# A quarter of the last stage's row gathers split in two by bounded indices, on one NeuronCore

## The chip, the cores and the metric

The kernel runs on one core of a Trainium2 chip. The metric is the device time of one launch in microseconds (us). A profiled execution also gives the span from the first to the last instruction. The core has TensorE (PE), VectorE (DVE), ScalarE (ACT), GpSimd (POOL) and SyncE (SP), and 16 DMA engines that all queues share.

## The reference

A two-layer transformer with dilated and windowed attention and expert-choice experts is followed by a second one of two layers, each with a mixer and a retrieval layer over 16,384 single-neuron experts. The part that matters here is that retrieval layer, in its second layer, for the second half of the 256 tokens:

```python
def peer_ffn(h, w_q, sub_keys, u, v):
    q = (h @ w_q).reshape(b, s, PEER_HEADS, 2, PEER_QDIM // 2)
    scores = jnp.einsum('bshic,ikc->bshik', q, sub_keys).astype(jnp.float32)
    top_s, top_i = lax.top_k(scores, PEER_TOPK)                 # 16 of 128 keys, twice
    ...
    cand_i = top_i[..., 0, :, None] * PEER_KEYS + top_i[..., 1, None, :]
    ...
    best_s, pos = lax.top_k(cand_s, PEER_TOPK)
    expert = jnp.take_along_axis(cand_i, pos, axis=-1)
    gate = jax.nn.softmax(best_s, axis=-1).astype(h.dtype)
    ...
        act = jax.nn.gelu(jnp.einsum('td,thkd->thk', xt, u[et]), approximate=False)
        return jnp.einsum('thk,thkd->td', act * gt, v[et])
```

Each token has 8 heads of 16 experts, that is 128 experts; an expert is a row of `u` and a row of `v`, 1024 floats each. An expert's number is `128 * a + b`, a and b being its two keys.

## The kernel before

The rows of `u` and `v` lie side by side in one tensor `puv` of 32,768 rows (16,384 of each layer) of 2048 floats, 8 KB. The 128 tokens of a tile stand on the 128 partitions. There are four gather stages, `(l, i)`: layer l, tile i. A stage handles 128 sets j. Set j is one row for each token, the row of its j-th expert: one indirect DMA issued by POOL brings 128 rows, 1 MB, with the row numbers in column j of `IX[:, i]`. For each set

- POOL (`gather`, L3167) waits until TensorE has used the buffer's former set (`.used`), and issues the gather;
- VectorE (L2465) waits for the landing (`g{l}{i}.{j}`) and multiplies the `u` half with the token's activations to one number;
- ScalarE (L2529) makes the gelu, times the gate, and spreads it over a diagonal matrix `dg`;
- TensorE (L1610) waits for `g` and `dg` and adds `dg` times the `v` half to the accumulators `acc` in four matmul instructions.

All four take the sets in the order of j. The sets go round through a `Ring` of buffers. At set 90 of the first stage the ring comes to hold buffers 0 to 7 alone, so that eight sets of 1 MB stand in turn in eight buffers from there on. Each buffer k has a semaphore `rows_landed[k]`.

The row numbers come from `route(l, i, q)`, 13 steps on VectorE between the sets of the quarter before; the row numbers of quarter q serve sets 32q to 32q+31. In the last stage `(1, 1)` its only side work is the routing of the next quarter and a short end of tile 0. After set 127 `final_last` adds the accumulators, normalises and stores. `did` adds to an engine's own semaphore, `land` sets up a DMA's landing as a name to wait for:

```python
                    k, before = rows.take(name)
                    G.wait_ge(*at[f"{before}.used"])
```

Of the kernel before, what the change touches and what calls it, by code (L numbers as in the profile page):

```python
# [6 lines left out]
U32 = mybir.dt.uint32  # L7
# [122 lines left out]
def program(nc, I, out):  # L130
    ctx = ExitStack()
    with ctx:
        def sb(name, shape, dt=F32):
            return ctx.enter_context(nc.sbuf_tensor(name, shape, dt))
# [11 lines left out]
        cbuf = sb("cbuf", [P, 2, 1536])  # L146
        ar = sb("ar", [P, 16384])
        bc = sb("bc", [P, 324])
        arU = ar[:, :].bitcast(U32)
        PS = [ctx.enter_context(nc.psum_tensor(f"ps{i}", [P, 512], F32)) for i in range(8)]  # L150
        zd = nc.dram_tensor("zd", (12, 128, 512), F32, kind="Internal").ap()
# [40 lines left out]
        def arv(a, b, pat=None, **k):  # L192
            v = ar[:, a:b]
            return v if pat is None else v.rearrange(pat, **k)
# [278 lines left out]


        GA = arv(6656, 6912, "p (i n) -> p i n", i=2)
        IX = arU[:, 6912:7168].rearrange("p (i n) -> p i n", i=2)
        DT = arv(7168, 7424, "p (i n) -> p i n", i=2)
        DG = arv(7424, 7936, "p (k n) -> p k n", k=4)
# [1156 lines left out]
        def vector_program(V):  # L1635
# [6 lines left out]
            def ts(o, i, s1, s2, op0, op1, *names):  # L1642
                if op1 is None:
                    V.did(V.e.tensor_scalar(o, i, s1, None, op0), *names)
                else:
                    V.did(V.e.tensor_scalar(o, i, s1, s2, op0, op1), *names)  # L1646
# [755 lines left out]
            def route(l, i, q):  # L2402
                p = f"rt{l}{i}{q}"
                yield
                yield
                V.wait_ge(*at[p + ".out"])
                for c in range(4):
                    top16(TS[:, c, :], TIU[:, c, :], SS[:, c, :], R2[:, 0:128])
                    yield
                copy(TIF, TIU, p + ".ss")  # L2410
                t4 = TS.rearrange("p (h i) n -> p h i n", i=2)
                tt(CA.rearrange("p h (a b) -> p h a b", a=16), t4[:, :, 0, :].unsqueeze(3).to_broadcast([P, 2, 16, 16]),
                   t4[:, :, 1, :].unsqueeze(2).to_broadcast([P, 2, 16, 16]), ALU.add)
                yield
                for h in range(2):
                    top16(BS[:, h, :], PO[:, h, :], CA[:, h, :], R2[:, 0:256])
                    yield
                gi = GA[:, i, 32 * q:32 * q + 32].rearrange("p (h n) -> p h n", h=2)
                tt(gi, BS, BS[:, :, 0:1].to_broadcast([P, 2, 16]), ALU.subtract, p + ".gi")
                ts(PQ[:, 0], PO, 4, None, ALU.logical_shift_right, None)  # L2420
                ts(PQ[:, 1], PO, 15, None, ALU.bitwise_and, None)
                copy(PQF, PQ)
                yield
                f4 = TIF.rearrange("p (h i) n -> p h i n", i=2)
                io = C("iota")[:, 0:16].unsqueeze(1).unsqueeze(1).to_broadcast([P, 2, 16, 16])
                e4 = EQ.rearrange("p (h k a) -> p h k a", h=2, k=16)
                for n in range(2):
                    tt(e4, PQF[:, n].unsqueeze(3).to_broadcast([P, 2, 16, 16]), io, ALU.is_equal)
                    tt(e4, e4, f4[:, :, n, :].unsqueeze(2).to_broadcast([P, 2, 16, 16]), ALU.mult)
                    red(I12[:, n], e4, ALU.add)  # L2430
                    yield
                stt(I12[:, 0], I12[:, 0], 128.0, I12[:, 1], ALU.mult, ALU.add)
                ts(IX[:, i, 32 * q:32 * q + 32].rearrange("p (h n) -> p h n", h=2), I12[:, 0], float(l * 16384), None,
                   ALU.add, None, p + ".ix")
                gates_of(p, gi)
                yield

# [681 lines left out]
        def pool_program(G):  # L3119
# [33 lines left out]
            def gather(l, i):  # L3153
                for j in range(128):
                    if (l, i, j) == (0, 0, 90):
                        for k in (10, 11):
                            rows.keep(k)
                        rows.release_first(6, 7)
                    if (l, i) == (0, 0) and j in (0, 16):
                        G.wait_ge(*at[f"rt000.ix{j // 16}"])  # L3160
                    elif j % 32 == 0:
                        G.wait_ge(*at[f"rt{l}{i}{j // 32}.ix"])
                    name = f"g{l}{i}.{j}"
                    k, before = rows.take(name)
                    G.wait_ge(*at[f"{before}.used"])
                    place[name] = k
                    G.land(G.e.indirect_dma_start(  # L3167
                        out=rows_of(name), out_offset=None, in_=I["puv"],
                        in_offset=bass.IndirectOffsetOnAxis(ap=IX[:, i, j:j + 1], axis=0)), rows_landed[k], count, name)
                    if (l, i) == (0, 0) and j in NEAR_AT:  # L3170
                        hp = NEAR_AT[j]
                        G.wait_ge(*at[f"ma1.bh{hp}"])
                        G.wait_ge(*at["ma1.mask"])
                        masked(1, hp, aB1[hp % 2])
# [179 lines left out]
```

## Time and profile before

| | |
|---|---|
| device time, median of 2 runs (lowest, highest) | 3018.68 us (3015.69, 3021.68) |
| span of the profiled execution | 3014.0 us |
| median less span | 4.7 us |
| busy: TensorE, VectorE, ScalarE, POOL | 82%, 47%, 29%, 23% |
| bytes moved, mean rate | 1103.07 MB, 366 GB/s |
| gathers: number, bytes, packets | 512, 536.90 MB, 73,728 |
| last gather issued, last instruction group | 2986.94 us, 3010.86 us |

The busy shares are means over the whole span. The time that the profiled execution itself took beside its span isn't recorded apart; the table sets the median against it. What the change touches lies in the last stage, which ends the kernel. It has 128 of the 512 gathers.

### The profile page before, as it was taken

To read this page: it belongs to the slowest core of one execution; us is meant where nothing else is said; L and a number is where in the kernel's file an instruction comes from. 1 tells how busy PE (TensorE), PEld (TensorE's weight loads), DVE (VectorE), ACT (ScalarE), POOL (GpSimd) and SP (SyncE) were. 2 spreads that over 40 slices of the span, in tenths; PEclk is the share of its full clock that TensorE was granted. 3 is DMA by queue.
4 is the path that set the end of the run, shared out by engine and by line. 5 is a ranking of instruction groups with operands and counts; after the bars stand their busy time and mean duration, and the time that the engine had idled before them with its cause. 6 is when DMAs were issued, how large, how long until landed. Compare 5 with 4: busy or idle time off the path is not lost.

```text
span 3014.0 us, 33710 instructions
## 1 busy us (share of the span) xinstructions
PE 2483.8 (82%) x11942; PEld 1357.6 (45%) x11942; DVE 1427.4 (47%) x3388; ACT 875.9 (29%) x2346; POOL 705.6 (23%) x626
## 2 busy tenths in 40 slices
PE   8999865657999966656798999898897988977777
PEld 8777311112978421212475445464462644632222
DVE  3363100002355201000448886687766787676674
ACT  0231100000022100000225554357334663344333
POOL 4020000001311000000014553334334334444442
PEclk9999978778999987888899999999999999999999
DMA  6337999999434899999929999999999999999997
GB/s 262 141 135 307 413 428 429 427 428 420 175 114 160 368 427 427 427 428 428 381 93 416 419 417 420 421 422 404 411 422 422 422 373 422 421 421 421 421 421 326
DMA packets 123511, 1103.07 MB, mean 366 GB/s; under 512 B 13744, under 2 KB 19280, under 8 KB 23760
## 3 DMA queue, kind: packets, MB, share of 16 engines
q1 hardware_dynamic: 47888, 560.88, 44.7%
q0 software_dynamic: 73728, 536.90, 43.2%
q10 hardware_dynamic: 1728, 3.14, 0.3%
q8 instruction: 95, 1.56, 0.2%
q14 instruction: 72, 0.59, 0.1%
HBM read 1096.68 MB, written 4.19 MB: 365 GB/s over the span
## 4 chain that ended last, share of the span: by engine, by line
PE 41%; DMA 41%; DVE 10%; issue 4%; ACT 3%; POOL 1%; SPq 0%; DVEq 0%; ACTq 0%
PE ps L771 17%; DMA wbuf<-in_puv,ar 17%; PE ps L1610 11%; DMA wbuf<-in_w_expert_up 9%; DMA wbuf<-in_w_expert_down 7%; DMA wbuf<-in_w_expert_gate 6%; PE ps L962 4%; PE ps L1142 3%; DVE wbuf L2465 3%; DMA wbuf<-in_w_mem_kv 2%; PE ps L927 2%; ACT ar L2529 2%; PE ps L775 1%; ACT L2529 1%; DVE ar L1640 1%
## 5 line engine op out<-in xcount | busy, mean ns | idle before, releaser
L1610 PE MATMUL ps<-wbuf,ar 128*128 128x512 f32 x1960 | 935.4, 617 | 181.5 <-ACT ar L2529 181.0
L2465 DVE CUSTOM_DVE_ANT_0 wbuf<-wbuf,Y 128x1024 f32<-128x1024 f32 x490 | 603.3, 1231 | 344.3 <-DMA wbuf<-in_puv,ar 335.4
L3167 POOL DMA_INDIRECT wbuf<-in_puv,ar x490 | 549.5, 1121 | 809.0 <-PE ps L1610 728.0
L1142 PE MATMUL ps<-wbuf,ar 128*32 128x512 f32 x2944 | 456.9, 757 | 288.3 <-DMA wbuf<-in_w_expert_up 112.5
L1610 PEld LDWEIGHTS ps<-wbuf,ar 128*128 128x128 f32 x1960 | 360.2, 195 | 674.1 <-issue 671.9
L2529 ACT ACTIVATE ar<-ar 128x1 f32<-128x1 f32 (+1 forms) x1051 | 269.5, 256 | 656.2 <-DVE ar L2465 635.0
L771 PE MATMUL ps<-HT,wbuf 128*128 128x128 f32 (+1 forms) x2640 | 411.3, 312 | 7.4 <-DMA wbuf<-in_w_mem_kv 5.9
L771 PEld LDWEIGHTS ps<-HT,wbuf 128*128 128x128 f32 x2640 | 373.3, 192 | 60.9 <-issue 26.6
L1142 PEld LDWEIGHTS ps<-wbuf,ar 128*32 128x32 f32 x2944 | 92.6, 125 | 639.3 <-issue 204.5
L2526 ACT COPY ar<-ps 128x512 f32<-128x512 f32 (+4 forms) x166 | 76.3, 460 | 705.8 <-PE ps L1142 304.0
L3126 POOL TENSOR_TENSOR sm<-sm,co 128x1 f32<-128x1 f32 x18 | 10.5, 583 | 1111.8 <-DVE sm L1646 1111.6
L1640 DVE TENSOR_TENSOR ar<-ar,ps 128x512 f32<-128x512 f32 (+1 forms) x20 | 13.2, 660 | 464.2 <-PE ps L1142 462.9
L2529 ACT ACTIVATE ar<-co,ar 128x128 f32<-128x128 f32 x512 | 205.6, 401 | 21.6 <-PE ps L1610 5.0
L1637 DVE COPY ar<-ps 128x512 f32<-128x512 f32 (+5 forms) x76 | 47.1, 620 | 335.5 <-PE ps L1142 270.4
L2529 ACT ACT_TABLE_LOAD x101 | 129.6, 1283 | 91.1 <-PE ps L1142 53.0
L3141 POOL TENSOR_TENSOR wbuf<-wbuf 128x512 f32<-128x512 f32 x20 | 26.2, 1308 | 343.9 <-DMA wbuf<-in_w_branch_b 214.1
L771 PE MATMUL ps<-ar 64*128 64x256 f32 (+3 forms) x508 | 97.3, 390 | 9.9 <-DVE ar L1637 7.1
L2529 ACT ACTIVATE ar<-ar,sm 128x257 f32<-128x257 f32 (+2 forms) x84 | 45.8, 545 | 163.1 <-issue 56.2
L771 PEld LDWEIGHTS ps<-ar 64*128 64x128 f32 (+1 forms) x508 | 55.8, 191 | 64.1 <-issue 41.3
L2529 ACT ACTIVATE ar<-ps 128x512 f32<-128x512 f32 (+2 forms) x43 | 20.8, 484 | 218.1 <-PE ps L1142 191.0
L771 PE MATMUL ps<-wbuf,HT 128*128 128x256 f32 (+1 forms) x384 | 83.4, 369 | 0.0
L962 PE MATMUL ps<-wbuf 128*128 128x128 f32 x640 | 77.9, 275 | 0.0
(208 smaller groups left out, 2089.6 us busy)
## 6 DMA issues: line engine op xcount, KB each, us to landing
wbuf<-in_w_expert_down SPq DMA_DIRECT2D x64, 2048.0 KB, 31.8
wbuf<-in_w_expert_up SPq DMA_DIRECT2D x62, 2048.0 KB, 31.4
wbuf<-in_w_expert_gate SPq DMA_DIRECT2D x58, 2048.0 KB, 30.7
wbuf<-in_w_in SPq DMA_DIRECT2D x20, 2048.0 KB, 9.0
wbuf<-in_peer_w_q SPq DMA_DIRECT2D x14, 2048.0 KB, 11.9
wbuf<-in_b_w_in SPq DMA_DIRECT2D x6, 2048.0 KB, 11.8
wbuf<-in_w_o SPq DMA_DIRECT2D x5, 2048.0 KB, 23.1
wbuf<-in_w_branch_b SPq DMA_DIRECT2D x4, 2048.0 KB, 7.6
```

What stands on the lines that cost most here:

```text
L771: m = T.e.matmul(o, l, r, start=(n == 0), stop=(n == len(pairs) - 1))
L775: return T.e.transpose(o, i, ident[0:i.shape[0], 0:i.shape[0]])
L927: m = T.e.matmul(b[:, :], lhs[:, c, 128 * i:128 * i + 128], v[:, c, :], start=(c == 0), stop=(c == 7))
L962: m = T.e.matmul(o, l[:, c, :], r[:, c, :], start=(start and c == 0), stop=(c == 3), skip_group_check=True)
L1142: m = T.e.matmul(ps(jobs[n])[32 * k:32 * k + 32, :], lhs(c, k), v[:, 512 * n:512 * n + 512], start=(c == 0), stop=(c == 7), tile_position= ...
L1610: m = T.e.matmul(acc[n][:, :], DG[:, j % 4, :], rows_of(name)[:, 1024 + 512 * n:1536 + 512 * n], start=(j == 0), stop=(j == 127))
L1637: V.did(V.e.tensor_copy(o, i), *names)
L1640: V.did(V.e.tensor_tensor(o, a, b, op), *names)
L2465: V.did(V.e.tensor_tensor_reduce(u, u, Y[:, i, :], 1.0, 0.0, ALU.mult, ALU.add, DT[:, i, j:j + 1]), f"dot{l}{i}.{j}")
L2526: A.did(A.e.copy(o, i), *names)
L2529: A.did(A.e.activation(o, i, f, **kw), *names)
L3167: G.land(G.e.indirect_dma_start(out=rows_of(name), out_offset=None, in_=I["puv"], in_offset=bass.IndirectOffsetOnAxis(ap=IX[:, i, j:j + 1] ...
```

## The change

Only stage `(1, 1)` changes. Its sets with j = 0, 4, 8, ... (32 of 128) are brought by two gathers into the same buffer. Both are given a bound, 32,767, with the order to leave out, without an error, a row whose number is above it. The first, "far", reads its numbers from `IX`, where 65,536 has been added to the rows whose second key b is below 24. The second reads them from `NX`, where 65,536 has been added to all others. So each row of the set comes by one of them. The other 96 sets come by one gather each, as before, with the true numbers, now in `FX`. `NX` and `FX` are columns of a new tile `near_ix`.

POOL issues in the order far j, j+1, j+2, near j, j+3. Ahead of near j it waits until far j has landed. The name `g11.j`, for which VectorE and TensorE wait, now stands for the landing of near j. The routing of the four quarters makes seven small results in place of one.

```diff
+        near_ix = sb("near_ix", [P, 256])
...
+        NX, FX = (near_ix[:, a:a + 128].bitcast(U32) for a in (0, 128))
...
                 stt(I12[:, 0], I12[:, 0], 128.0, I12[:, 1], ALU.mult, ALU.add)
-                ts(IX[:, i, 32 * q:32 * q + 32].rearrange("p (h n) -> p h n", h=2), I12[:, 0], float(l * 16384), None,
-                   ALU.add, None, p + ".ix")
+                ix = IX[:, i, 32 * q:32 * q + 32].rearrange("p (h n) -> p h n", h=2)
+                if (l, i) == (1, 1):
+                    ts(FX[:, 32 * q:32 * q + 32].rearrange("p (h n) -> p h n", h=2), I12[:, 0], 16384.0, None, ALU.add, None)
+                    far = R2[:, 0:32].rearrange("p (h n) -> p h n", h=2)
+                    ts(far, I12[:, 1], 24.0, 65536.0, ALU.is_lt, ALU.mult)
+                    tt(I12[:, 1], I12[:, 0], far, ALU.add)
+                    ts(ix, I12[:, 1], 16384.0, None, ALU.add, None)
+                    ts(far, far, -1.0, 65536.0, ALU.mult, ALU.add)
+                    tt(I12[:, 1], I12[:, 0], far, ALU.add)
+                    ts(NX[:, 32 * q:32 * q + 32].rearrange("p (h n) -> p h n", h=2), I12[:, 1], 16384.0, None, ALU.add, None,
+                       p + ".ix")
+                else:
+                    ts(ix, I12[:, 0], float(l * 16384), None, ALU.add, None, p + ".ix")
...
                     place[name] = k
...
+                    if (l, i) == (1, 1) and j % 4 == 0:
+                        late = (j, k, name)
+                        G.land(G.e.indirect_dma_start(
+                            out=rows_of(name), out_offset=None, in_=I["puv"],
+                            in_offset=bass.IndirectOffsetOnAxis(ap=IX[:, i, j:j + 1], axis=0),
+                            bounds_check=32767, oob_is_err=False), rows_landed[k], count, name + ".far")
+                        continue
+                    if (l, i) == (1, 1):
+                        G.land(G.e.indirect_dma_start(
+                            out=rows_of(name), out_offset=None, in_=I["puv"],
+                            in_offset=bass.IndirectOffsetOnAxis(ap=FX[:, j:j + 1], axis=0)), rows_landed[k], count, name)
+                        if j % 4 == 2:
+                            j0, k0, first = late
+                            G.wait_ge(*at[first + ".far"])
+                            G.land(G.e.indirect_dma_start(
+                                out=rows_of(first), out_offset=None, in_=I["puv"],
+                                in_offset=bass.IndirectOffsetOnAxis(ap=NX[:, j0:j0 + 1], axis=0),
+                                bounds_check=32767, oob_is_err=False), rows_landed[k0], count, first)
```

On POOL, a quarter of the last stage stands like this before; L3167 is the gather, `tensor_done` the wait for the buffer, `vector_done` that for the row numbers:

```order
L3167 DMA wbuf<-in_puv,ar 128x2048 [waits tensor_done,vector_done]
L3167 DMA wbuf<-in_puv,ar 128x2048 [waits tensor_done] x31
L3167 DMA wbuf<-in_puv,ar 128x2048 [waits tensor_done,vector_done]
L3167 DMA wbuf<-in_puv,ar 128x2048 [waits tensor_done] x31
L3167 DMA wbuf<-in_puv,ar 128x2048 [waits tensor_done,vector_done]
```

The same place afterwards, in the midst of a quarter; L3182 is a far gather, L3188 a whole one, L3194 a near one:

```order
L3182 DMA wbuf<-in_puv,ar 128x2048 [waits tensor_done]
L3188 DMA wbuf<-in_puv,near_ix 128x2048 [waits tensor_done] x2
L3194 DMA wbuf<-in_puv,near_ix 128x2048 [waits rows_landed2]
L3188 DMA wbuf<-in_puv,near_ix 128x2048 [waits tensor_done]
L3182 DMA wbuf<-in_puv,ar 128x2048 [waits tensor_done]
L3188 DMA wbuf<-in_puv,near_ix 128x2048 [waits tensor_done] x2
L3194 DMA wbuf<-in_puv,near_ix 128x2048 [waits rows_landed0]
```

Each four sets have five gathers, and the fourth of them stands behind a wait for a landing.

On VectorE, at the end of a routing, the row numbers before; L2465 is a set's product (two rows each), L1649 joins the two keys, L1652 begins the gates:

```order
L2465 ISA wbuf,ar<-wbuf,Y 128x1024 [waits rows_landed1,vector_done]
L2465 ISA ar 128x1
L1649 SCALAR_TENSOR_TENSOR ar<-ar 128x32 [waits vector_done]
L1644 TENSOR_SCALAR ar<-ar 128x32 [waits vector_done]
L1652 TENSOR_REDUCE sm<-ar 128x2 [waits scalar_done,vector_done]
```

and afterwards:

```order
L2478 ISA wbuf,ar<-wbuf,Y 128x1024 [waits rows_landed1,vector_done]
L2478 ISA ar 128x1
L1651 SCALAR_TENSOR_TENSOR ar<-ar 128x32 [waits vector_done]
L1646 TENSOR_SCALAR near_ix<-ar 128x32 [waits vector_done]
L1648 TENSOR_SCALAR ar<-ar 128x32 [waits vector_done]
L1642 TENSOR_TENSOR ar<-ar 128x32 [waits vector_done]
L1646 TENSOR_SCALAR ar<-ar 128x32 [waits vector_done]
L1648 TENSOR_SCALAR ar<-ar 128x32 [waits vector_done]
L1642 TENSOR_TENSOR ar<-ar 128x32 [waits vector_done]
L1646 TENSOR_SCALAR near_ix<-ar 128x32 [waits vector_done]
L1654 TENSOR_REDUCE sm<-ar 128x2 [waits scalar_done,vector_done]
```

Six instructions more stand there, four times in the kernel. The orders of TensorE, ScalarE and SP have no other row than before.

## Rows read from the trace of the kernel before

**Rows 1.** The page: DMA share and GB/s, 40 slices; transfer queues.

```profile
DMA  6337999999434899999929999999999999999997
GB/s 262 141 135 307 413 428 429 427 428 420 175 114 160 368 427 427 427 428 428 381 93 416 419 417 420 421 422 404 411 422 422 422 373 422 421 421 421 421 421 326
...
q0 software_dynamic: 73728, 536.90, 43.2%
```

**Rows 2.** Engines in 260 us of the last gather stage.

```profile
core 0: us, PE busy (x) PEld busy (x) DVE busy (x) ACT busy (x) POOL busy (x), PEclk, DMA share, GB/s
2700.00:2960.00 260.00, 198.18 (x429) 73.27 (x430) 180.65 (x395) 102.41 (x321) 112.00 (x105) 1.00 1.01 421
```

**Rows 3.** Chain that ended last, last stage, one turn of the buffers.

```profile
2962.40 1.29 DVE wbuf L2465
...
2963.79 0.21 ACT ar L2529
...
2964.35 0.41 ACT ar L2529
...
2964.90 1.97 PE ps L1610 x4
...
2967.12 15.02 DMA wbuf<-in_puv,ar
```

**Rows 4.** Gathers of the last stage: durations, then issue to landing.

```profile
L3167 POOL DMA_INDIRECT wbuf<-in_puv,ar x116: 932/939/1985, 2698.3 to 2986.9; - x116
...
  PE ps L1610: 161.8, 102
  issue: 4.0, 13
...
DMA to landing us min/median/max: 13.6/15.1/16.1
```

**Rows 5.** Timeline of POOL, last quarter of the last stage.

```profile
start us, us, engine line op out<-in xcount [idle before <-releaser]
...
2937.27 0.94 POOL L3167 DMA_INDIRECT wbuf<-in_puv,ar  x1 [1.56 <-PE ps L1610]
2939.75 0.94 POOL L3167 DMA_INDIRECT wbuf<-in_puv,ar  x1 [1.54 <-PE ps L1610]
```

**Rows 6.** First and fifth gather of a burst into an empty queue.

```profile
L3167 POOL DMA_INDIRECT wbuf<-in_puv,ar x1: 1125/1125/1125, 1573.4 to 1573.4; - x1
...
DMA to landing us min/median/max: 5.7/5.7/5.7
...
L3167 POOL DMA_INDIRECT ar<-in_puv,ar x1: 937/937/937, 1578.7 to 1578.7; - x1
...
DMA to landing us min/median/max: 11.8/11.8/11.8
```

**Rows 7.** Three gathers issued into a thin queue, stage before.

```profile
L3167 POOL DMA_INDIRECT wbuf<-in_puv,ar x3: 939/941/1039, 2476.8 to 2481.0; - x3
...
DMA to landing us min/median/max: 6.6/7.6/7.7
```

**Rows 8.** Timeline at the end: last set, last products.

```profile
2986.94 0.94 POOL L3167 DMA_INDIRECT wbuf<-in_puv,ar  x1 [1.49 <-PE ps L1610]
...
3002.02 1.22 DVE L2465 CUSTOM_DVE_ANT_0 wbuf<-wbuf,Y 128x1024 f32<-128x1024 f32 x1 [1.23 <-DMA wbuf<-in_puv,ar]
...
3003.35 0.53 ACT L2529 ACTIVATE ar<-ar 128x1 f32<-128x1 f32 x2 [1.49 <-DVE ar L2465]
3003.91 0.40 ACT L2529 ACTIVATE ar<-co,ar 128x128 f32<-128x128 f32 x1
...
3004.45 1.96 PE L1610 MATMUL ps<-wbuf,ar 128*128 128x512 f32 x4 [0.50 <-ACT ar L2529]
...
3006.52 1.41 DVE L1640 TENSOR_TENSOR X<-X,ps 128x512 f32<-128x512 f32 x2 [3.26 <-PE ps L1610]
```

**Rows 9.** VectorE groups of the last stage by shape.

```profile
L1644 DVE TENSOR_SCALAR ar<-ar 128x32 uint32<-128x32 uint32 x6 | 1.4, 231 | 0.2
...
L1640 DVE TENSOR_TENSOR ar<-ar 128x32 f32<-128x32 f32 x3 | 0.6, 192 | 0.1
...
L1644 DVE TENSOR_SCALAR ar<-ar 128x32 uint32<-128x32 f32 x3 | 0.5, 181 | 0.1
```

**Rows 10.** TensorE before, where its clock had fallen; then those stretches.

```profile
2472.71 5.37 PE L1610 MATMUL ps<-wbuf,ar 128*128 128x512 f32 x8 [1.71 <-ACT ar L2529]
...
2472.00:2473.00 1.00, 0.29 (x1) 0.30 (x2) 0.96 (x3) 0.90 (x4) 0.00 (x0) 0.98 1.02 434
2473.00:2474.00 1.00, 1.00 (x2) 0.34 (x1) 0.93 (x4) 0.90 (x4) 0.00 (x0) 0.50 1.14 352
2476.00:2477.00 1.00, 1.00 (x3) 0.53 (x2) 1.00 (x2) 0.00 (x0) 0.17 (x1) 0.81 0.58 221
```

More of the change, by code:

```diff
@@ L3166, in gather @@
                     place[name] = k
-                    G.land(G.e.indirect_dma_start(
-                        out=rows_of(name), out_offset=None, in_=I["puv"],
-                        in_offset=bass.IndirectOffsetOnAxis(ap=IX[:, i, j:j + 1], axis=0)), rows_landed[k], count, name)
+                    if (l, i) == (1, 1) and j % 4 == 0:
[16 more added lines that the diff above has]
+                                bounds_check=32767, oob_is_err=False), rows_landed[k0], count, first)
+                    else:
+                        G.land(G.e.indirect_dma_start(
+                            out=rows_of(name), out_offset=None, in_=I["puv"],
+                            in_offset=bass.IndirectOffsetOnAxis(ap=IX[:, i, j:j + 1], axis=0)), rows_landed[k], count, name)
                     if (l, i) == (0, 0) and j in NEAR_AT:
```

## The prediction

> **What bounds the kernel now.** I read the page's rows of transfers first. Over the last tenth the DMA engines are full in nearly every slice, at 421 GB/s [rows 1]. The windows of the last stage then say whether that is its limit: the DMA share is 1.01, TensorE is busy 198 of 260 us with its clock at 1.00, VectorE 181 and POOL 112 [rows 2]. So a set costs what its bytes cost: 1,048,576 B at 421 GB/s is 2.49 us, and POOL's issues do stand 2.48 us apart [rows 5]. The chain shows how this closes into a ring: gather issued, 15.0 us to landing, product on VectorE 1.29, ScalarE 0.21 and 0.41 with a small gap, TensorE 1.97, next gather [rows 3]. From that product's start (2962.40) to the gather (2967.12) are 4.7 us, and with the 15.0 such a turn takes 19.7 us: eight sets of 2.48. POOL waits for TensorE 102 times, 161.8 us in all [rows 4]: it stands behind the buffers, not the buffers behind it. Of the 15.1 us from issue to landing the transfer is 2.49, so that most of it is queue. A gather into an empty queue landed after 5.7 us [rows 6]. The cover of the stage, the time by which an issue may be late without an idle DMA engine, is thus about 15.1 - 5.7 = 9.4 us.
>
> **What the change does to the transfers.** The bytes stay the same if a row that is left out moves nothing. With b spread evenly over 128 keys (my assumption), 24/128 of a split set, 0.19, comes late: 0.47 us of transfer for near and 2.02 for far. The transfers already fill the engines, so nothing here can shorten them; I exclude a gain beyond run-to-run spread. What may be added is four things.
>
> First, **more gathers**, 160 in place of 128. A gather has 73,728 / 512 = 144 packets, 16 more than its 128 rows [rows 1]. What these 16 and the gather's end cost can't be seen alone. The nearest rows are rates: loads of 2 MB run at 428 GB/s, gathers of 1 MB at 421 [rows 1], or 2.45 against 2.49 us for 1 MB. If all of that difference is the gather's own cost, it is 0.04 us, and 32 more cost 1.3 us.
>
> Second, **the wait for far j**. Here the cover goes. Call W the time when far j has landed. Then only j+1 and j+2 are in the queue. Without a gap the landings would come at W+2.5 (j+1), W+5.0 (j+2), W+5.4 (near j), W+7.9 (j+3), W+10.0 (far j+4): a group of four takes 9.96 us. POOL's smallest gap between two gathers is 0.30 us and a gather takes it 0.94 [rows 4, 6]. So near j starts at W+0.3, j+3 at W+1.5, far j+4 at W+2.8, j+5 at W+4.0, j+6 at W+5.3. Their buffers are free by then: set j-4, the latest to become complete, had its near part landed 4.5 us before W and needs 2.5 us to TensorE [rows 3] and 2 us there; from there TensorE frees one buffer each 2 us. The critical one is j+3, issued 6.4 us before it should land. The fastest landing on record is 5.7 us, from an empty queue [rows 6]; into a thin queue three took 6.6, 7.6 and 7.7 [rows 7]. With 5.7 there is no loss. With 6.6 it is 0.2 us, with 7.7 it is 1.3 us a group. POOL's own time adds to it: its gathers take 0.94 us at the median but up to 1.99 [rows 4], and the mean, 112.00 us for 105 in the window, is 1.07 [rows 2]. Two issues stand on the path after W, so +0.3. I take the fastest of the thin queue, since j+1 and j+2 still run when j+3 is issued, and the mean of POOL: 0.2 + 0.3 = 0.5 us a group, 32 x 0.5 = 16 us. From both sides: 0, and the burst of rows 6. There the fifth gather, issued 5.3 us after the first, landed 11.4 us after it, so four landings took 11.4 for 9.96, 1.4 us lost a group, 46 us in all. A bounded gather may also take POOL longer than 0.94; nothing shows it. Each 0.1 us more in near costs up to 3 us.
>
> On the fixed part of a DMA the trace says that it lies under the queue while there is one: 5.7 us alone, 2.49 in a row [rows 2, 6]. The Trainium skill, page "DMA: Bandwidth & Descriptors", section "Anatomy of one DMA — SWDGE (gpsimd) path", fits a DMA as about 2.0 us plus its bytes over 436 GB/s, most of the first in the receipt of the last write. Its section "Rules for kernel authors" asks for 1 MiB in a DMA and for small ones to be joined, which speaks against this change. If those 2.0 us lay bare for each added gather, they would be an estimated 64 us in place of my 16 + 1.3; rows 2 speak against that as long as gathers queue.
>
> Third, **the order of completion**. VectorE and TensorE take the sets in order, so j, j+1, j+2 are all taken after near j lands, one set late for j+1, two for j. TensorE needs 4 x 1.96 = 7.8 us in 9.96 [rows 8] and catches up within the group. At the end there is no later group. Before, the last set's product starts at 3002.02, the matmuls at 3004.45 and end at 3006.41, 4.4 us later [rows 8]. Now near 124 lands one set, 2.49 us, ahead of set 127, and four sets have still to pass: -2.49 + 2.43 + 4 x 1.96 = 7.8. The tail grows by 3.4 us.
>
> Fourth, **24 small VectorE instructions** of 32 columns, 0.18 to 0.23 us each [rows 9], 5 us in all, six at a time. VectorE is idle 79 of 260 us [rows 2]; behind them are queued one product and the gates. The row numbers are wanted when the buffer of 8 sets before is free; they are made at the 26th set of a quarter and wanted for the 33rd, whose buffer is that of the 25th: about when POOL, after its new wait, reaches that set. The six, 1.2 us, fit in the 2.8 us that stand between W and far j+4. Cost 0. Were that cover gone, four times 1.2.
>
> Sum: 3014.0 + 1.3 + 16 + 3.4 = 3034.7 us of span. The median of the runs stands 4.7 above the span of before. Predicted: **3039 us**.
>
> **The rivals.**
>
> *The queue never runs thin.* If a loaded queue hands j+3 through like the empty one, only 1.3 + 3.4 remain: 3014.0 + 4.7 + 4.7 = 3023 us. For it: 5.7 us as lowest; against it: rows 7, and POOL's long issues.
>
> *Each group starts as from an empty queue.* Then the burst's 46 us: 3014.0 + 1.3 + 46 + 3.4 + 4.7 = 3069. For it: far j, being the slowest engine's landing, leaves the engines that had few of its rows ahead, with even less queued. Against: two whole sets are in the queue at W.
>
> *A left-out row costs like one that is brought* (slower than 2%). The place is the DMA queue, in each split set: its 128 rows are handled twice. Price 32 x 2.49 = 80 us: 3023 + 80 = 3103, more with thin queues. It passes 2% (60 us) as soon as, with my other 20.7, a left-out row costs half a whole one. No row shows a left-out row, for or against. I count with it the case in which the fixed part lies bare: by the two rates it is 32 x (5.7 - 2.49) = 103 us at the utmost, 3014.0 + 103 + 3.4 + 4.7 = 3125, and the skill's 2.0 us gives an estimate of 3086.
>
> *TensorE becomes the bound through its clock.* After an idle of 1.71 us the granted clock fell to 0.50 (of 2.4 GHz, so 1.2) for about 3 us, and two sets took 5.37 in place of 3.92 [rows 10]. The change gathers TensorE's gaps of half a us, now four in a group, into one of about 2 us. One such spell a group gives 7.8 + 1.5 = 9.3 us, still under 9.96, so it costs only its part in the tail, 1.5 us. If it stayed low throughout, 15.7 us a group, 32 x 5.7 = 182 us: 3200. Against: with two sets and more at hand, TensorE runs without a gap, and the clock was back at 1.00 within 4 us there.
>
> **How the numbers follow.** Thin queue with a loss of 0.2 to 1.2 us a group (3029 to 3062): 0.52, its middle at 3039. Never thin (3017 to 3029): 0.22. As from empty (3062 to 3079): 0.10. Over 3079 (left-out rows or bare fixed parts 0.13, clock 0.02): 0.15. Faster: 0.01. To leave out no more than 2 in 10 the range goes from 3020, where only 1.3 and a part of the tail remain, to 3080, past the burst's bound. 2%, 60 us, is about what a measurement of this kernel can tell from no change: faster by more 0.01, within 0.84, slower by more 0.15.
>
> **What would show it.** POOL's waits of the last stage: in each group one for a landing, before the near gather, of some 3 us, and a burst of five issues after it. The last stage at 400 to 421 GB/s and under 100% share if the loss is 0.5 us; at 421 with 32 x 2.49 us more length if left-out rows are moved (the bytes tell it too: 134 MB for the stage, or 168). The issue to landing of j+3: 6 to 7 us if I am right. The time from the last landing to the last matmul: 4.4 us for set 127 alone, 7.8 now after near 124. The near gather's own time on POOL: if it is over 1.5 us, I am too low. I would be wrong altogether if a bounded gather were handled by POOL in quite another way than these, or if TensorE's clock fell in each group for long.

## The result: 2.1% slower

The changed kernel takes 3081.72 us (median; 3078.46 to 3084.97), the one before 3018.68. The ratio is 1.0209, with a 95% interval of 1.0174 to 1.0244: 63 us more (53 to 74). It lies just over the forecast's range. The span of the profiled execution is 3076.6 us, 62.6 more than before.

The page of the changed kernel, its transfers (answering to [rows 1]):

```profile
DMA  6337999998335899999659999999999999999997
GB/s 264 131 144 308 429 428 428 428 427 364 148 137 232 370 427 428 427 428 428 242 228 421 418 422 422 421 416 408 413 422 419 410 396 422 403 356 345 361 342 281
...
DMA packets 128121, 1103.11 MB, mean 359 GB/s; under 512 B 18352, under 2 KB 23888, under 8 KB 28368
...
q0 software_dynamic: 78336, 536.92, 43.4%
...
HBM read 1130.24 MB, written 4.19 MB: 369 GB/s over the span
```

and the line of packets before:

```profile
DMA packets 123511, 1103.07 MB, mean 366 GB/s; under 512 B 13744, under 2 KB 19280, under 8 KB 23760
```

Slices 36 to 39 have lost rate, 342 to 361 GB/s where 421 stood. The software queue carries 536.92 MB, 0.02 MB more than before, in 4,608 packets more, 144 for each of the 32 new gathers: a gather has as many packets as before, however many of its 8 KB rows it leaves out. The packets under 512 B are more by the same 4,608. The queue brings none of the left-out rows in full. Yet the count of bytes read from HBM is 1096.68 MB on the page before and 1130.24 here, 33.56 MB more, as if each left-out row had been read.

The window of 260 us in the last stage (columns as in [rows 2]):

```profile
2700.00:2960.00 260.00, 183.55 (x367) 75.80 (x368) 165.41 (x389) 88.21 (x274) 117.16 (x108) 0.89 0.94 352
```

The DMA share has fallen from 1.01 to 0.94, the rate from 421 to 352, the granted clock from 1.00 to 0.89. The engines of the transfers are no longer full, and no compute engine has filled up in their place. POOL's waits in the last stage from 2696 us on (engine, what it issues, for whom: us in all, times, longest):

```profile
POOL wbuf L3194 <- DMA wbuf<-in_puv,ar: 159.8, 30, 6.1
POOL wbuf L3188 <- issue: 22.9, 75, 0.3
...
POOL wbuf L3188 <- PE ps L1612: 4.6, 15, 0.3
```

Before, it waited for TensorE 102 times, 161.8 us, in about the same stretch [rows 4]. Now it waits for far j (L3194 is the near gather), 5.3 us a time, and hardly for TensorE. The ring is no longer closed through the buffers but through the wait for a landing.

### The profile page after: what moved, and what is told of

It reads as the page before. It is cut to its first block, busy times and chain, and to the rows that moved or that the text cites. A ratio compares the mean times of both kernels' runs of the same rounds, so it can differ in the third digit from the quotient of the medians.

```text
span 3076.6 us, 33830 instructions
## 1 busy us (share of the span) xinstructions
PE 2507.6 (82%) x11942; PEld 1379.6 (45%) x11942; DVE 1427.8 (46%) x3412; ACT 875.7 (28%) x2346; POOL 743.5 (24%) x658
## 3 DMA queue, kind: packets, MB, share of 16 engines
q0 software_dynamic: 78336, 536.92, 43.4%
HBM read 1130.24 MB, written 4.19 MB: 369 GB/s over the span
## 4 chain that ended last, share of the span: by engine, by line
DMA 44%; PE 39%; DVE 8%; issue 5%; ACT 3%; POOL 1%; SPq 0%; DVEq 0%; POOLq 0%; ACTq 0%
DMA wbuf<-in_puv,ar 19%; PE ps L773 16%; PE ps L1612 9%; DMA wbuf<-in_w_expert_up 8%; DMA wbuf<-in_w_expert_down 8%; DMA wbuf<-in_w_expert_gate 5%; PE ps L964 4%; PE ps L1144 3%; DMA wbuf<-in_w_mem_kv 2%; DVE wbuf L2478 2%; PE ps L929 2%; ACT ar L2542 1%; PE ps L777 1%; DMA wbuf<-in_puv,near_ix 1%; ACT L2542 1%
## 5 line engine op out<-in xcount | busy, mean ns | idle before, releaser
L1612 PE MATMUL ps<-wbuf,ar 128*128 128x512 f32 x1960 | 953.0, 633 | 219.3 <-ACT ar L2542 218.9
L1612 PEld LDWEIGHTS ps<-wbuf,ar 128*128 128x128 f32 x1960 | 377.4, 202 | 712.0 <-issue 710.1
L3199 POOL DMA_INDIRECT wbuf<-in_puv,ar x362 | 409.5, 1131 | 619.4 <-PE ps L1612 558.5
L3188 POOL DMA_INDIRECT wbuf<-in_puv,near_ix x96 | 105.2, 1096 | 29.3 <-issue 24.1
L2542 ACT ACTIVATE ar<-ar,sm 128x257 f32<-128x257 f32 (+2 forms) x84 | 45.8, 546 | 161.8 <-issue 55.5
```

What stands on the lines that cost most here:

```text
L1612: m = T.e.matmul(acc[n][:, :], DG[:, j % 4, :], rows_of(name)[:, 1024 + 512 * n:1536 + 512 * n], start=(j == 0), stop=(j == 127))
L2542: A.did(A.e.activation(o, i, f, **kw), *names)
L3188: G.land(G.e.indirect_dma_start(out=rows_of(name), out_offset=None, in_=I["puv"], in_offset=bass.IndirectOffsetOnAxis(ap=FX[:, j:j + 1], a ...
L3199: G.land(G.e.indirect_dma_start(out=rows_of(name), out_offset=None, in_=I["puv"], in_offset=bass.IndirectOffsetOnAxis(ap=IX[:, i, j:j + 1] ...
```

## What one group of four costs now

W is, as in the prediction, the time when far j has landed. The chain that ended last, at one such wait (start, us, what):

```profile
2922.85 8.57 DMA wbuf<-in_puv,ar
...
2931.44 0.03 POOLq L3194
2931.47 0.73 issue
2932.20 4.79 DMA wbuf<-in_puv,near_ix
```

Far j is issued at 2922.85 and lands at 2931.42. The wait is met at once (POOLq at 2931.44), but near starts at 2932.20, 0.78 us after the landing. Then the timeline of POOL at another wait:

```profile
2908.35 1.05 POOL L3194 DMA_INDIRECT wbuf<-in_puv,near_ix  x1 [4.66 <-DMA wbuf<-in_puv,ar]
2909.70 0.95 POOL L3188 DMA_INDIRECT wbuf<-in_puv,near_ix  x1 [0.30 <-issue]
2910.96 0.99 POOL L3182 DMA_INDIRECT wbuf<-in_puv,ar  x1 [0.30 <-issue]
```

Near takes 1.05 us, and j+3 starts 1.35 us behind near; over the 25 groups from 2700 to 3000 it is 1.46. So j+3 starts 0.78 + 1.46 = 2.2 us after W. How long it is on its way (the gather of 2909.70, its duration in ns, then issue to landing):

```profile
L3188 POOL DMA_INDIRECT wbuf<-in_puv,near_ix x1: 947/947/947, 2909.7 to 2909.7; - x1
...
DMA to landing us min/median/max: 7.7/7.7/7.7
```

Read in the same way, the 32 gathers j+3 take 5.4 to 8.3 us, 7.4 in the mean. They land 9.6 us after W, where 7.9 would do without a gap. The 32 far gathers (durations, first and last start), then issue to landing of the first and of the last:

```profile
L3182 POOL DMA_INDIRECT wbuf<-in_puv,ar x32: 995/999/1979, 2667.1 to 3043.6; - x32
...
DMA to landing us min/median/max: 13.5/13.5/13.5
...
DMA to landing us min/median/max: 8.0/8.0/8.0
```

The first lands at 2667.1 + 13.5 = 2680.6, the last at 3043.6 + 8.0 = 3051.6. 31 groups between them give 11.97 us a group, 2.0 more than the 9.96 of four sets at the full rate. By the mean distances of landings: j+2 to near 0.45 (forecast 0.47), near to j+3 4.15 (for 2.49), j+3 to far j+4 2.37 (for 2.02), the other two together 5.0 (for 4.98). So 1.7 us go where j+3 is late, and 0.35 at its neighbour.

That the 31 x 2.0 = 62 us equal the whole change is in part chance, since the kernel before did not keep to 9.96 either. Its sets 0 and 124 of the stage (duration, start, then issue to landing):

```profile
L3167 POOL DMA_INDIRECT wbuf<-in_puv,ar x1: 939/939/939, 2666.8 to 2666.8; - x1
...
DMA to landing us min/median/max: 14.5/14.5/14.5
...
L3167 POOL DMA_INDIRECT wbuf<-in_puv,ar x1: 935/935/935, 2979.8 to 2979.8; - x1
...
DMA to landing us min/median/max: 14.7/14.7/14.7
```

They land at 2681.3 and 2994.5: 10.10 us for four sets. Against that the 31 groups lose 1.87 us each, 58 us. The end adds about the rest: the last set lands 10.3 us after far 124, where it landed 7.3 us after set 124 before, and then comes the longer tail.

At the end VectorE and TensorE (answering to [rows 8]):

```profile
3057.81 1.23 DVE L2478 CUSTOM_DVE_ANT_0 wbuf<-wbuf,Y 128x1024 f32<-128x1024 f32 x1 [6.38 <-DMA wbuf<-in_puv,near_ix]
...
3060.25 8.80 PE L1612 MATMUL ps<-wbuf,ar 128*128 128x512 f32 x16 [4.79 <-ACT ar L2542]
...
3062.08 1.23 DVE L2478 CUSTOM_DVE_ANT_0 wbuf<-wbuf,Y 128x1024 f32<-128x1024 f32 x1 [0.49 <-DMA wbuf<-in_puv,near_ix]
...
3069.16 1.41 DVE L1642 TENSOR_TENSOR X<-X,ps 128x512 f32<-128x512 f32 x2 [5.85 <-PE ps L1612]
```

From the last product's start to the accumulators' addition are 7.1 us, 4.5 before: 2.6 more. Two things differ from the forecast's tail. The last set's product starts 4.3 us after that of set 124, where 2.5 were foretold, which leaves less to do after it; and the 16 matmuls of four sets take 8.80 us, where 7.84 were foretold.

## The experiments

All stand beside runs of the kernel before on the same chip. Differences in us are the ratio's, times 3015.

### The wait alone

```diff
                         in_offset=bass.IndirectOffsetOnAxis(ap=IX[:, i, j:j + 1], axis=0)), rows_landed[k], count, name)
+                    if (l, i) == (1, 1) and j % 4 == 2:
+                        G.wait_ge(*at[f"g11.{j - 2}"])
```

> The kernel before, all sets of the last stage by one whole gather, and only the new wait: at each third set of four (j % 4 = 2) POOL waits until set j-2 has landed, so that two sets are left in the queue, 32 times. No bounds, no second gather. Theory A (thin queue and left-out rows each cost about half of the 63 us): 30 to 40 us over before, 3050 to 3058. Theory B (the thin queue alone costs it): about 60 us, 3079. Theory C (the left-out rows alone): under 6 us, up to 3025.

Measured: 3036.37 us, ratio 1.007 (1.0053 to 1.0087), 21 us more. That is under theory A's 30 to 40 and far from B and C. The window of 300 us has a share of 0.99 and 393 GB/s, where the same window of the kernel before has 1.00 and 415:

```profile
2700.00:3000.00 300.00, 224.25 (x467) 82.72 (x467) 191.40 (x412) 110.20 (x347) 133.06 (x112) 0.97 0.99 393
```

The chain at a wait tells a part of the difference:

```profile
2872.79 8.50 DMA wbuf<-in_puv,ar
2881.29 0.26 issue
2881.55 7.34 DMA wbuf<-in_puv,ar
```

Set j lands at 2881.29, and the next gather starts 0.26 us later, not 0.78. A plain gather behind the wait starts half a us sooner than the bounded one of the changed kernel. And here it is j+3 itself, with no near ahead of it.

### The same wait with three sets in the queue

```diff
+                    if (l, i) == (1, 1) and j % 4 == 3:
+                        G.wait_ge(*at[f"g11.{j - 3}"])
```

> As the run with two sets left in the queue, but the wait stands one set later (j % 4 = 3, for set j-3), so that three sets, 7.5 us of transfer, are left when POOL goes on. If the loss comes of a gather's 5.7 to 7.7 us from issue to landing being longer than what is queued (theories A and B), three sets cover it: under 6 us over before, up to 3025. If it comes of the wait itself, whatever is queued: as with two sets left.

Measured: 3016.78 us, ratio 1.0003 (0.9993 to 1.0013), no change. The rate is back at 416 GB/s, with the share at 1.01:

```profile
2700.00:3000.00 300.00, 230.68 (x495) 84.29 (x493) 200.02 (x426) 116.58 (x369) 136.81 (x116) 1.00 1.01 416
```

So the wait costs nothing measurable by itself. It costs what the queue behind it doesn't cover: with two sets (5.0 us) 21 us, with three (7.5 us) none.

### The left-out rows alone

```diff
+                if (l, i) == (1, 1):
+                    ts(OX[:, 32 * q:32 * q + 32].rearrange("p (h n) -> p h n", h=2), I12[:, 0], 81920.0, None, ALU.add, None)
...
+                    if (l, i) == (1, 1) and j % 4 == 0:
...
+                            t = wbuf[:, shape["row_tiles"][4], 2048 * (m % 2):2048 * (m % 2) + 2048]
+                            G.land(G.e.indirect_dma_start(
+                                out=t, out_offset=None, in_=I["puv"],
+                                in_offset=bass.IndirectOffsetOnAxis(ap=OX[:, j + x:j + x + 1], axis=0),
+                                bounds_check=32767, oob_is_err=False), rows_landed[8 + m % 2], count, f"idle{m}")
```

> The kernel before, with 32 gathers more in the last stage, one ahead of each fourth set's successor, that leave out all their 128 rows; they go to buffers that nobody reads and no one waits for them but the same buffer's next, 20 us later. So the queue stays deep. VectorE makes four more index columns of 32. Theory A: 0.9 us each, by the landings of the first group after the change, 25 to 35 us over before, 3044 to 3054. Theory B: only the gather's end, 0.04 us each, 1 to 2 us, 3020. Theory C: 60 us, 3079.

Measured: 3018.42 us, ratio 1.0005 (0.9995 to 1.0014): 1.5 us, at most 4.2, for 4,096 rows left out in 32 gathers beside a deep queue. Theories A and C fall. Rows brought would have cost 80 us. A window of the last stage:

```profile
2700.00:2900.00 200.00, 152.46 (x333) 56.73 (x331) 146.92 (x338) 79.72 (x246) 110.59 (x100) 1.00 1.02 418
```

The packets (78,336) and the HBM count (1130.24 MB) are those of the changed kernel, the rate is 418 GB/s for 421: 0.7% of 9.96 us, 0.07 us a gather. The same run with rows of 1 KB asks what the HBM count counts:

> As the run with 32 gathers that leave out all rows beside a deep queue, but of rows of 256 floats (1 KB) in place of 2048. One look, for the page's count of bytes read from HBM: with rows of 8 KB it stood 33.56 MB over before. If a row left out is counted by its length: 4.2 MB over before. If by a fixed size: 33.6 MB again. The time: within 4 us of before by either.

One execution took 3014.3 us. Its page:

```profile
q0 software_dynamic: 75264, 536.92, 43.3%
...
HBM read 1100.88 MB, written 4.19 MB: 367 GB/s over the span
```

1100.88 less 1096.68 is 4.2 MB: 4,096 rows of 1 KB, as 33.56 MB are 4,096 of 8 KB. The count goes by the row's length, but the time doesn't: a row left out stands in the page's HBM count and is next to free here. The gathers have 48 packets each there (75,264 less 73,728, over 32), not 144, so that the number of packets goes by the row's length too. Whether the bytes of a left-out row are read at all is not shown by this. The page's count alone would have misled me to a transfer of 80 us.

### One more gather alone

```diff
+                    if (l, i) == (1, 1) and j % 4 == 0:
+                        for h in range(2):
+                            G.land(G.e.indirect_dma_start(
+                                out=rows_of(name)[:, 1024 * h:1024 * h + 1024], out_offset=None,
+                                in_=I["puv"].rearrange("r (h n) -> (r h) n", h=2),
+                                in_offset=bass.IndirectOffsetOnAxis(ap=HX[:, j:j + 1], axis=0),
+                                element_offset=1024 * h), rows_landed[k], count, name if h else None)
+                        continue
```

> The kernel before, with the same 32 sets brought by two gathers each, but of half rows (columns 0 to 1023, then 1024 to 2047) of all 128 tokens, issued one behind the other with no wait and no bound. It measures what one more gather costs in a deep queue: by the two rates of rows 1, 0.04 us each, 1 to 2 us, 3017 to 3022; if its 2.0 to 3.2 us lay bare, 64 to 100 us.

Measured: 3016.94 us, ratio 1.0007 (0.9997 to 1.0016), 2 us more (-1 to 5), 0.07 us a gather, which agrees with the forecast's 0.04 within the interval. What one more gather costs by itself is covered by the deep queue here.

### The time that POOL spends between the wait and the next whole gather

```diff
+        spent = sb("spent", [P, 320])
...
+                    if (l, i) == (1, 1) and j % 4 == 2:
+                        G.wait_ge(*at[f"g11.{j - 2}"])
+                        G.did(G.e.tensor_tensor(spent[:, :], C("causal")[:, 0:320], C("causal")[:, 0:320], ALU.add))
```

> The run with two sets left in the queue at the wait (21 us over before), and behind each wait one POOL instruction (an addition of 320 columns into a tile that nobody reads) in the place where the change has the near gather, so that set j+1's follower in the ring is issued about 1.2 us later. No bounds, no second gather. Theory D (what costs is the time from W to the next whole gather, 0.3 us in that run, 1.5 us after the change; each us later than the cover is lost): 21 + 32 x 1.2 = 55 to 62 us over before, 3070 to 3077. Theory E (the left-out rows cost little beside a deep queue, but about 1 us in a thin one): 21 to 30 us, up to 3045.

Measured: 3082.5 us, ratio 1.022 (1.0203 to 1.0237), 66 us more, the loss of the changed kernel and a little over it, with no bound, no split set and no row left out. The chain at a wait:

```profile
2868.60 5.16 issue
2873.76 0.02 POOLq L84
2873.78 0.02 issue
2873.80 0.73 POOL spent L3173
2874.53 0.26 issue
2874.79 1.64 POOL wbuf L3168
```

The instruction takes 0.73 us and puts the gather 1.03 us behind the landing, where 0.26 stood; and the gather behind it takes 1.64 us. Together its end is later by 0.77 + 0.13 (the mean of that gather was 1.51 in the run with the wait alone, 1.65 here), and the second gather takes longer too (1.13 and 1.52). It costs 45 us more than the wait alone, 1.4 a group. The 66 us in all are just over theory D's 55 to 62: the wait and a delay behind it cost as much as the whole change. But the size of the loss doesn't follow from the delay. In the mean the whole gather starts 1.1 us behind the landing here and 2.2 in the changed kernel, at about the same loss.

The second run puts a gather that leaves out all its rows in the addition's place:

```diff
+                    if (l, i) == (1, 1) and j % 4 == 2:
+                        G.wait_ge(*at[f"g11.{j - 2}"])
...
+                            G.land(G.e.indirect_dma_start(
+                                out=t, out_offset=None, in_=I["puv"],
+                                in_offset=bass.IndirectOffsetOnAxis(ap=OX[:, j + x:j + x + 1], axis=0),
+                                bounds_check=32767, oob_is_err=False), rows_landed[8 + m % 2], count, f"idle{m}")
```

> As the run with two sets left, and behind each wait a gather that leaves out all its 128 rows, into a buffer that nobody reads. It has the change's POOL time and more left-out rows than near (128 for 104), but brings none and splits no set. Theory D: 55 to 62 us over before, as with the POOL instruction. Theory E: the POOL part is small and the rest comes here, so that this is 30 us or more over the run with the POOL instruction. Only if both hold would it pass 75 us.

Measured: 3065.61 us, ratio 1.0163 (1.0146 to 1.018), 49 us more. That is just under theory D's 55 to 62, and 17 us under the run with the POOL instruction, where theory E wanted 30 over it. Left-out rows are not dear in a thin queue either. POOL in the window of 260 us (out<-in, count, busy, mean ns, idle before):

```profile
L3172 POOL DMA_INDIRECT wbuf<-in_puv,ar x91 | 95.4, 1048 | 27.7 <-issue 26.5 <-PE ps L1612 1.2
L3186 POOL DMA_INDIRECT wbuf<-in_puv,out_ix x22 | 31.5, 1430 | 105.6 <-DMA wbuf<-in_puv,ar 105.6
```

The gather that leaves out all takes POOL 1.43 us, and still its place costs less than the addition of 0.72. Its followers are short (1.05 in the mean, 1.32 in the run with the addition). So what POOL does in the place matters also for how long its next gathers take, on POOL and on their way. From 2700 to 2980 the first whole gather starts 2.5 us after the landing here and lands 5.8 us later in the mean; behind the addition it starts at 1.1 us and needs 8.2. Why, these runs don't settle, and no price per us of delay comes out of them.

Nor do they give all of the changed kernel's loss. There j+3 starts at 2.2 us and needs 7.4, with the same two sets and near ahead of it. This run has the wait, the bounded gather and left-out rows, and costs 49 us; the change costs 63, of which 2.6 are the tail. The other 11 or so lie within the two intervals (44 to 54 and 53 to 74), so that the times alone don't show them, but the 1.5 us between the two times to landing point the same way. What near's rows do to j+3 in a thin queue is not shown.

### The near gather one set later

```diff
-                        if j % 4 == 2:
+                        if j % 4 == 3 - j // 124:
```

> The changed kernel with the wait for far j and near j one set later, after j+3 in place of after j+2 (near 124 still after 126): three sets are left in the queue. All left-out rows and the eight buffers stay. Theories D and E: three sets cover the 1.5 us and the landing; 5 to 12 us over before (the tail, 5 us, and the left-out rows), 3021 to 3028. If the split as such costs, whatever is queued: over 3050.

Measured: 3052.7 us, ratio 1.0127 (1.011 to 1.0143), 38 us more: better than the changed kernel by 25, but not the 5 to 12 expected. POOL's waits, and the window of 300 us:

```profile
POOL wbuf L3194 <- DMA wbuf<-in_puv,ar: 49.2, 17, 4.7
POOL wbuf L3188 <- PE ps L1612: 47.8, 56, 1.7
POOL wbuf L3182 <- PE ps L1612: 41.8, 18, 4.2
```

```profile
2700.00:3000.00 300.00, 220.71 (x441) 90.87 (x442) 192.30 (x433) 107.43 (x336) 147.80 (x133) 0.88 0.96 376
```

TensorE has come back as the one waited for, 90 us, 74 times. The sets behind near j are held until it lands, a set later than after the change, and with them their buffers. I hadn't counted that. Two runs ask for its two parts, the number of buffers and TensorE's clock:

```diff
+                if (l, i) == (1, 1):
+                    for qj in range(4):
+                        G.wait_ge(*at[f"p11.wq{qj}.used"])
+                    rows.release_first(8, 9)
```

> The changed kernel with near j after j+3 (38 us over before with eight buffers, where POOL then waited for TensorE), and now ten buffers in the ring of the last stage. Theory F (three sets would cover the landing, but the sets held back behind near j keep the eight buffers full, so that the next gathers wait for TensorE): two buffers more take that away; 8 to 18 us over before, 3023 to 3033. Theory G (the split itself costs in a deep queue too): stays at 30 to 40 us.

Measured: 3023.54 us, ratio 1.0029 (1.0019 to 1.004), 9 us more. The window has a share of 1.01 and 410 GB/s:

```profile
2700.00:3000.00 300.00, 233.20 (x485) 95.55 (x485) 205.14 (x456) 116.23 (x367) 158.81 (x146) 0.93 1.01 410
```

POOL's waits for TensorE are down to 22 us, of which the profile puts 12 to the near gather (L3198), whose own wait is for far j:

```profile
POOL wbuf L3198 <- PE ps L1612: 11.9, 5, 2.7
POOL wbuf L3192 <- PE ps L1612: 9.8, 17, 1.2
```

Here every split set, near gather, left-out row and wait of the change is in place, with three sets left in the queue and ten buffers, and 54 us of the 63 are gone. What stays is what the longer tail and the gathers cost in the forecast, 4.7 us, and about 4 more.

```diff
+                        if (l, i) == (1, 1) and j % 4 == 0:
+                            busy(f"fill{j}", 16)
                         T.wait_ge(*at[name])
```

> The changed kernel with near j after j+3 and eight buffers (38 us over before), and ahead of each wait for a split set TensorE turns the identity 16 times into a bank that nobody reads (about 3 us), so that it isn't idle before the four sets that come at once. If the half clock after its idle time is what makes the buffers late: the granted clock of the last stage rises from 0.85 to 0.90 to 0.97 or more, and the time falls by 10 to 20 us, to 3033 to 3043. If the buffers are late for their order alone: within 5 us of the run without it, 3047 to 3057.

Measured: 3040.94 us, ratio 1.0083 (1.0064 to 1.0101), 25 us more, 13 less than without the filling. The clock is 0.97 for 0.88:

```profile
2700.00:3000.00 300.00, 255.73 (x895) 134.57 (x894) 196.17 (x441) 110.47 (x348) 156.84 (x139) 0.97 0.98 389
```

So of the 38 us with eight buffers about a third was the half clock after TensorE's idle time.

### The near gather after the next far one, with ten buffers

```diff
-                        late = (j, k, name)
+                        early, late = late, (j, k, name)
...
+                        if early:
+                            j0, k0, first = early
+                            G.wait_ge(*at[first + ".far"])
```

> The changed kernel, but near j is issued, and far j waited for, after far j+4 in place of after j+2 (near 124 still after 126), with ten buffers in the ring in place of eight in the last stage. Four sets are left in the queue at each wait. The left-out rows are all there. Theory A: the left-out rows' part stays, 29 us, and the longer tail, 5 us: 3048 to 3056. Theory B: 3 to 8 us over before, 3022 to 3027. Theory C: as the changed kernel, 3075 to 3082.

Measured: 3032.27 us, ratio 1.0048 (1.0031 to 1.0065), 14 us more, between theories A and B; the run with the left-out rows alone has since ruled out A. What it holds instead:

```profile
POOL wbuf L3200 <- PE ps L1612: 77.1, 43, 4.3
...
POOL wbuf L3187 <- DVE ar L1642: 12.3, 3, 4.8
```

```profile
3013.41 15.67 PE L1612 MATMUL ps<-wbuf,ar 128*128 128x512 f32 x32 [2.72 <-ACT ar L2542]
```

With ten buffers, the first gather of a quarter asks for its row numbers two sets sooner, before VectorE has made them: 12.3 us in three waits. And at the end eight sets stand behind near 120 and 124, so that TensorE has 15.67 us of matmuls in one piece after the data. POOL waits for TensorE 77 us ahead of whole gathers (L3200), and the window from 2700 to 3000 us has 395 GB/s where the one with near one set later and ten buffers has 410. How the 14 us divide among these three is not shown. Four sets in the queue are more than is needed, and cost their own.

To issue near j with no wait at all, behind far j, was not tried: both write the same buffer, and only the indices say that they write different rows.

## Why the prediction was wrong

**The bound, right.** The transfers bound the stage before, and near's 0.47 (0.45 measured) holds. The 9.96 us of a group is the rate without its interruptions; the kernel before took 10.10 in the mean.

**More gathers, right.** 1.3 us were foretold for 32; the halves cost 2 (-1 to 5), the gathers that leave all out 1.5 (-1.5 to 4.2). The Trainium skill ("DMA: Bandwidth & Descriptors", "Anatomy of one DMA — SWDGE (gpsimd) path") gives a DMA about 2.0 us of fixed cost; the halves show that the deep queue covers it here. My estimate of 64 us from that figure, and with it the 3086 of a rival, come close to the measured 63 and 3082, but not by its reason. An added gather without the wait costs next to nothing, the wait without an added gather costs 21 us, and with three sets left and ten buffers the same DMAs leave 9.

**The wait for far j, wrong in size.** The step that failed is "I take the fastest of the thin queue, since j+1 and j+2 still run when j+3 is issued, and the mean of POOL: 0.2 + 0.3 = 0.5 us a group, 32 x 0.5 = 16 us." It measured 2.0 us a group, 62 us. Two terms of it were too small, and one was missing. The start of j+3 was W+1.5 in the forecast, +0.3 for POOL's long gathers; it was W+2.2, since near starts 0.78 us after the landing, not 0.30. That is 0.4 us more. The 0.30 was read between gathers that follow one another, and says nothing of how long a bounded one takes to start behind a wait. And from issue to landing I took 6.6 us, the best of three rows, where the 32 show 7.4, 0.8 us more. With the 0.5 foretold that makes the 1.7 lost at j+3. The 0.35 at far j+4 was not in the forecast. The 7.7 that I had put beside it as the other value of [rows 7] was the nearer one, and gave 1.3 + 0.3 = 1.6 us a group. That would have been 51 us, 3074 in all. The mechanism, and the place, were as described: the burst of five after each wait, and the loss at j+3. Why j+3 needs 7.4 us on its way, where it needs 5.8 behind a gather that leaves out all its rows, stays open.

**The bound from the other side, wrong.** I took the burst into an empty queue, 1.4 us a group, for the worst, and so ended the range at 3080. After the change a small gather stands ahead of the first whole one, which the burst of [rows 6] has not. The bound should have had near's start and its time on POOL added.

**The tail, right in kind.** It is +2.6 us for a forecast of 3.4, by two errors that partly cancel: the last set came 4.3 us after near 124, not 2.5 (-1.8), and the matmuls took 8.80 us, not 7.84 (+1.0), with a part at half clock.

**VectorE's 24 instructions, right.** In the whole stage POOL waits once for row numbers, 3.0 us ahead of its first far gather, while its queue is still full (that gather takes 13.5 us to land); before it was once, 3.1 us.

**The rivals.** "The queue never runs thin" is what the version with near one set later and ten buffers comes to: 3024 measured, 3023 foretold. "A left-out row costs like one that is brought" is out beside a deep queue: 0.05 us for 128 rows; behind the wait its gather costs less than an addition of 0.72 us. The sign that I had named for it, 33.6 MB more, did appear in the count of bytes read from HBM, and it was a wrong sign: the queue's own bytes and the time don't have them. TensorE's clock did fall, in most groups: the 0.88 over 300 us makes an estimated 72 us at half clock, 2.9 a group. TensorE in one group, and the stretch in steps of 1 us:

```profile
2916.10 8.80 PE L1612 MATMUL ps<-wbuf,ar 128*128 128x512 f32 x16 [3.43 <-ACT ar L2542]
...
2917.00:2918.00 1.00, 1.00 (x3) 0.53 (x2) 0.97 (x2) 0.22 (x1) 0.00 (x0) 0.64 1.05 418
2918.00:2919.00 1.00, 1.00 (x2) 0.34 (x1) 0.96 (x3) 0.49 (x2) 0.00 (x0) 0.50 0.99 418
```

TensorE had been idle for 3.43 us, longer than the 2 us that I gave it, and the 16 matmuls took 8.80 us, under the 9.3 foretold. POOL waited for TensorE 4.6 us in all, so that this was free within the stage, as argued. It begins to cost once the buffers bind: 13 us in the version with near one set later.

## What to carry to other kernels

A wait for a landing on the issuing engine costs what the queue behind it does not cover. Count from the landing: the engine's start after the wait, everything it issues ahead of the next large transfer, and that transfer's full time to landing in a thin queue; take the middle of the rows, not the best. Even the middle is only a guide: between three runs with two whole sets ahead, that time was 5.8, 7.4 and 8.2 us. Here two 1 MB gathers (5.0 us) were too few and three (7.5 us) enough, as long as the buffers sufficed; sets that are completed late hold their buffers, and the depth has to grow with that.

## What the runs showed of the hardware that I had not expected

- A bounded gather behind a met wait starts 0.78 us after the landing (0.74 to 0.83 in the 32 near gathers), a plain one 0.26. Behind another gather both start after 0.30.
- The first gather behind a met wait is long on POOL, bounded or not: 1.51 us in the mean for a plain one, 1.43 for one that leaves out all, 1.14 for near, where 0.94 is the median of the kernel before [rows 4].
- A gather that leaves out all its rows of 8 KB has the same 144 packets as a whole one, adds its rows' full length to the page's count of bytes read from HBM, and costs 0.05 us beside a deep queue.
- A POOL addition of 320 columns ahead of the gathers cost more (45 us for 32) than a gather of 1.43 us in the same place (28 us). The whole gather behind the addition took POOL 1.65 us in the mean and 8.2 to land, the one behind the gather 1.05 and 5.8.
